# A hybrid decoder layer on one core: one part of the conditioning projection computed at another place, recurrent outputs kept token-major, and the last stage rebuilt

## What is computed

```python
sh1, sc1, g1, sh2, sc2, g2 = split(silu(c) @ w_ada + b_ada)   # six rows of 2048 for each of 9 conditioning vectors
u  = x * (1 + sc1) + sh1
hq, hf, hi, hg, sq, sk, sv = split(u @ w_in)                  # 8 heads of 128 in each group of 1024
o_h, state = hgrn2(silu(hq), f, 1 - f, hi)                    # recurrent heads, 32-token chunks in the kernel
o_h = rms_norm(o_h, hg_norm) * silu(hg)                       # mean square over the 128 values of a head
o_s = rms_norm(stick_breaking(sq, sk, sv, cache), sb_norm)
x1 = LayerNorm(ALPHA * x + g1 * (concat(o_h, o_s) @ w_o))
u2 = x1 * (1 + sc2) + sh2
y  = LayerNorm(ALPHA * x1 + g2 * experts(u2))                 # two of 32 SwiGLU experts for each token
```

## Time and profile before

| | |
|---|---|
| median of 3 runs | 1797.02 us (1795.12 to 1797.27) |
| the profiled execution | 1795.09 us, of which the span from first to last instruction is 1793.3 us |
| TensorE busy (matmuls) | 1591.6 us, 89% of the span |
| VectorE, ScalarE, GpSimd busy | 562.4, 183.6 and 115.3 us |
| moved by DMA | 536.87 MB, mean 299 GB/s |
| granted TensorE clock, mean | 0.951 of full speed |

### The profile page before, as it was taken

One profiled execution on the slowest core, in us unless ns is written; L12 is line 12 of the kernel. 1 busy time (PEld: TensorE's weight loads), 2 busy tenths in 40 slices (PEclk: granted clock), 3 DMA queues, 4 the chain that ended last, 5 costly groups with the idle time before them and its releaser, 6 DMA issues.

```text
span 1793.3 us, 24360 instructions
## 1 busy us (share of the span) xinstructions
PE 1591.6 (89%) x9319; PEld 964.3 (54%) x9319; DVE 562.4 (31%) x988; ACT 183.6 (10%) x298; POOL 115.3 (6%) x154
## 2 busy tenths in 40 slices
PE   3679999999999999999958999999999998999871
PEld 0036666634777775567744646464655454545440
DVE  0010009641221224431466132323232313232328
ACT  0000001300000013321025100000000000000002
POOL 3000000000111100000020000000000000000004
PEclk8789999999998989999988999999999999999995
DMA  9998788875442334465424799999999999999961
GB/s 352 421 381 333 308 333 306 325 283 233 131 142 88 130 120 155 142 250 205 141 94 159 314 420 421 421 421 421 421 421 420 421 421 420 421 421 421 420 263 53
DMA packets 82878, 536.87 MB, mean 299 GB/s; under 512 B 11491, under 2 KB 11667, under 8 KB 24018
## 3 DMA queue, kind: packets, MB, share of 16 engines
q1 hardware_dynamic: 74450, 507.62, 70.8%
q0 software_dynamic: 8048, 26.28, 4.4%
q10 hardware_dynamic: 336, 2.36, 0.4%
HBM read 532.87 MB, written 11.80 MB: 304 GB/s over the span
## 4 chain that ended last, share of the span: by engine, by line
PE 64%; DMA 25%; DVE 6%; issue 3%; ACT 1%; SPq 1%; DVEq 0%; ACTq 0%
DMA ring<-w_up 20%; PE ps L607 18%; PE ps L1071 11%; PE ps L863 7%; PE ps L615 6%; DMA ring<-w_ada 5%; PE ps L1090 5%; PE ps L591 4%; PE ps L1053 2%; PE ps L757 1%; PE ps L719 1%; PE ps L622 1%; DVE arena L1851 1%; SPq L386 1%; PE ps L738 1%
## 5 line engine op out<-in xcount | busy, mean ns | idle before, releaser
L1071 PE MATMUL ps<-ring,arena 128*64 128x256 f32 x3200 | 355.1, 380 | 9.9 <-DMA ring<-w_up 7.7
L607 PE MATMUL ps<-arena,ring 128*128 128x288 f32 x1280 | 325.2, 413 | 0.0
L1071 PEld LDWEIGHTS ps<-ring,arena 128*64 128x64 f32 x3200 | 266.8, 137 | 103.4 <-DMA ring<-w_up 18.4
L607 PEld LDWEIGHTS ps<-arena,ring 128*128 128x128 f32 x1280 | 242.9, 192 | 91.1 <-issue 25.5
L1090 PE MATMUL ps<-arena 128*64 128x512 f32 x800 | 177.2, 594 | 23.5 <-DVE arena L1862 23.5
L591 PE MATMUL ps<-ring,silu_c 128*32 128x512 f32 x768 | 113.2, 698 | 56.3 <-DMA ring<-w_ada 30.7
L1090 PEld LDWEIGHTS ps<-arena 128*64 128x64 f32 x800 | 66.2, 137 | 118.4 <-issue 90.5
L1053 PE MATMUL ps<-arena 64*128 64x512 f32 x400 | 108.1, 636 | 24.1 <-DVE arena L1851 14.9
L863 PE MATMUL ps<-arena,ring 128*128 128x288 f32 x512 | 125.5, 407 | 0.0
L1858 DVE TENSOR_TENSOR arena<-arena,ps 128x256 f32<-128x256 f32 x25 | 10.5, 422 | 342.4 <-PE ps L1071 342.4
L615 PE MATMUL ps<-ring,arena 128*128 128x512 f32 x256 | 114.6, 595 | 1.3 <-DVE arena L1430 1.3
(11 more groups left out here) (400 smaller groups left out, 1220.9 us busy)
## 6 DMA issues: line engine op xcount, KB each, us to landing
ring<-w_gate SPq DMA_DIRECT2D x100, 1024.0 KB, 23.5
ring<-w_up SPq DMA_DIRECT2D x100, 1024.0 KB, 26.4
arena<-w_down SPq DMA_DIRECT2D x100, 1024.0 KB, 20.3
ring<-w_ada SPq DMA_DIRECT2D x96, 1024.0 KB, 8.7
ring<-w_in SPq DMA_DIRECT2D x56, 1024.0 KB, 6.4
ring<-w_o SPq DMA_DIRECT2D x32, 512.0 KB, 6.6
ring<-cache_k SPq DMA_DIRECT2D x16, 512.0 KB, 3.8
ring<-cache_v SPq DMA_DIRECT2D x16, 512.0 KB, 4.0
```

The costliest lines, as they stand in the source:

```text
L607: last = mm(ps[:, bank, 0:T], ring[:, slot, P * t:P * (t + 1)], uT[:, t, :], start=(t == 0), stop=(t == KC - 1))
L1071: last = mm(ps[B * s:B * (s + 1), 2 + c // 4, 0:256], xgT[:, 4 * (c % 4) + t, :], ring[:, c, 512 * t + 256 * s:512 * t + 256 * (s + 1)], s ...
```

## The change

- **g2 moved.** The sixteen chunks of w_ada's sixth part leave the loop of stage 1. SP loads them after w_o's chunks, ahead of expert 0's; TensorE multiplies eight of them after the first LayerNorm's sums, four after the router, four after u2 is turned (`g2_chunks`). The bias rows `bg2` are loaded later. The four pairs of `select_g2` become one run of eight products after the gather lists, with 64 and 32 weight columns instead of 128 and 32.
- **Recurrent outputs token-major.** Queries are now the weights (32 columns in column strip 32*c4), states and values the moving side, into banks 6 and 2. ACT squares with accumulation (`hsum`), DVE scales to `otok`, and TensorE turns the result (`turn_out`): half 0's in the first pass of half 1, half 1's between the key tiles. `heads_out` on DVE applies norm weight and gate. The normalisation leaves the stick-breaking passes.
- **End rebuilt.** The sums start from ALPHA * x1 instead of zero; a block's output is multiplied by g2 when it leaves PSUM (DVE, two products a block; ACT copies both halves unscaled for the sample rows). The last block is taken out of the loop on each engine: its gate and up chunks 0 to 3, then `combine` of the block before, then chunks 4 to 7, down, and a spreading of its own, whose adds also give row sums; ACT gives the sums of squares about a mean guessed before. Sample tokens stay in four quadrants to the end. ln2's rows are loaded by SP behind the last weights, and SP issues the eight stores.

The diff, cut to its core (removed lines mostly left out, since the functions before stand above):

```diff
+        N_MIX, N_SQ, N_SV, N_V = 2 * KC, 2 * KC + 80, 2 * KC + 96, 2 * KC + 112
+        N_G2 = N_V + 24
+        N_END = N_G2 + KC
...
+            for c in range(SLOTS):
+                put(used(N_ROWS + c - SLOTS), c, w_in[3, c])
...
+            for t in range(KC):
+                put(used(N_G2 + t - SLOTS), t % SLOTS, w_ada[5, t])
...
+            sp.wait_ge(u2_stored, 3 * 16)
+            sp.dma_start(ln2b, ln2.partition_broadcast(P)).then_inc(late_loaded, 16)
...
+            pool.wait_ge(hnorm_dve, 6)
+            for j in range(4):
+                pool.dma_start(bg2[32 * j:32 * j + 32, :], b_g2[j].partition_broadcast(32)).then_inc(bg2_loaded, 16)
...
-                for t in (2 * c, 2 * c + 1):
-                    n = N_MIX + 3 * MIX + 3 * c + t % 2
-                    ada_chunk(n % SLOTS, loaded(n), t, 5)
-                n = N_MIX + 3 * MIX + 3 * c + 2
+                n = N_ROWS + c
...
+            def turn_out(half):
+
+                for tt in range(2):
+                    pe.wait_ge(htok_dve, 3 * half + tt + 1)
+                    for h in range(4):
+                        last = nc.tensor.transpose(ps[:, (6, 2)[tt], P * h:P * (h + 1)], otok[tt][:, h, :], ident[:])
+                    last.then_inc(hturn_pe, 1)
+                pe.wait_ge(htok_dve, 3 * half + 3)
+                nc.tensor.transpose(ps[:, 3, P:2 * P], osr, ident[:]).then_inc(hturn_pe, 1)
...
+                        if half == 1:
+                            turn_out(0)
...
+                    if half == 1 and c == 0:
+                        pe.wait_ge(hnorm_dve, 3)
...
+                pe.wait_ge(u_dve, 8 * half + 8)
+                for tt in range(2):
+                    for h in range(4):
+                        k = heads[h]
+                        o = ps[:, (6, 2)[tt], P * h:P * (h + 1)]
+                        for c4 in range(4):
+                            mm(o[CH * c4:CH * (c4 + 1)], abuf[:, tt, k, CH * c4:CH * (c4 + 1)],
+                               tok[:, 3 + tt, P * k:P * (k + 1)], start=True, stop=(4 * tt + c4 == 0),
+                               tile_position=(0, CH * c4))
+                        for c4 in range(4):
+                            c = 4 * tt + c4
+                            if c == 0:
+                                continue
+                            last = mm(o[CH * c4:CH * (c4 + 1)], hq[:, k, CH * c:CH * (c + 1)], shist[:, c - 1, h, :],
+                                      start=False, stop=True, tile_position=(0, CH * c4))
                     last.then_inc(hgo_pe, 1)
...
                 if i == 2:
+                    turn_out(1)
...
+                    pe.wait_ge(hnorm_dve, 6)
                 else:
-                    pe.wait_ge(hrs_act, c)
+                    pe.wait_ge(z_dve, c)
...
-                pe.wait_ge(z_dve, c + 1)
-                pe.wait_ge(hsq_act, c + 1)
-                mm(ps[:, 2, 0:T], ones[:], hsq, start=True, stop=True).then_inc(hrms_pe, 1)
...
+            def g2_chunks(ts):
+
+                for t in ts:
+                    ada_chunk(t % SLOTS, loaded(N_G2 + t), t, 5)
+
+            pe.wait_ge(ss_dve, 5)
+            g2_chunks(range(8))
+
...
+            g2_chunks(range(8, 12))
             for n in range(12):
                 turn_tokens(n, u2T)
+            g2_chunks(range(12, KC))
...
-            for j in range(2, 4):
-                select_g2(j)
-
...
+            pe.wait_ge(tt_act, 24)
+            pe.wait_ge(rows_copied, 6)
+            for j in range(4):
+                r = slice(32 * j, 32 * j + 32)
+                h = j // 2
+                mm(ps[B * h:B * (h + 1), 6 + j % 2, :], rowsel[r, 0:B], ada_rows[r, :], start=True, stop=True,
+                   tile_position=(32 * j, B * h))
+                last = mm(ps[r, 5, :], rowsel[r, P:P + TS], ada_rows[r, :], start=True, stop=True,
+                          tile_position=(32 * j, 32 * j))
+            last.then_inc(g2_pe, 1)
...
-                with pe.If(i < nblocks):
+                with pe.If(i < last_block):
...
+            pe.wait_ge(x_copied, nblocks)
+            for c in range(8):
+                gate_or_up(c, last_block)
+                if c == 3:
+                    combine(last_block)
+            turn_hidden(last_block)
+            for q in range(4):
+                pe.wait_ge(moe_loaded[8 + q], last_block * 16 + 16)
+                for nn in range(2):
+                    last = down(q, nn)
+                    if q == 3:
+                        last.then_inc(last_down, 1)
...
+            def last_tile(i, nn, banks):
+                for r in range(2):
+                    rows = slice(B * r, B * (r + 1))
+                    last = mm(ps[:, banks[r], :], spread[rows, P * i:P * (i + 1)], yout[rows, 512 * nn:512 * (nn + 1)],
+                              start=True, stop=True, tile_position=(B * r, 0))
+                last.then_inc(last_comb, 1)
...
+            pe.wait_ge(last_dve, 1)
+            last_tile(0, 0, (0, 1))
+            last_tile(1, 0, (2, 3))
+            pe.wait_ge(last_act, 2)
...
+            pe.wait_ge(last_dve, 2)
+            last_tile(0, 1, (6, 7))
+            pe.wait_ge(last_sum, 1)
+            last_tile(1, 1, (0, 1))
...
+                act.wait_ge(os_pe, 4 * (half + 1))
+                if half == 1:
+                    act.wait_ge(htok_dve, 3)
+                A(osr, ps[:, 3, 0:P], ACT.Square, accum_out=hsum[:, 2, 0:1])
+                for tt in range(2):
+                    act.wait_ge(hgo_pe, 2 * half + tt + 1)
+                    for h in range(4):
+                        last = A(otok[tt][:, h, :], ps[:, (6, 2)[tt], P * h:P * (h + 1)], ACT.Square,
+                                 accum_out=hsum[:, tt, h:h + 1])
+                    link(last)
+                    n = 4 if tt == 0 else 5
+                    s = hsum[:].rearrange("p a b -> p (a b)")[:, 4 * tt:4 * tt + n]
+                    link(A(s, s, ACT.Ln, bias=epsr[:, 0:1], scale=1.0 / P))
+                    A(s, s, ACT.Exp, scale=-0.5).then_inc(hsum_act, 1)
...
-                act.wait_ge(hrms_pe, c + 1)
-                if c >= 1:
-                    act.wait_ge(hnorm_dve, c)
-                link(A(hrs, ps[:, 2, 0:T], ACT.Ln, bias=epsr[:, 0:1], scale=1.0 / P))
-                A(hrs, hrs, ACT.Exp, scale=-0.5).then_inc(hrs_act, 1)
...
+            act.wait_ge(g2_pe, 1)
+            nc.scalar.copy(g2h, ps[:, 6:8, :].rearrange("p a n -> p (a n)"))
+            nc.scalar.copy(g2q, ps[:, 5, :]).then_inc(g2_act, 1)
...
+            act.wait_ge(tt_act, 24)
+            for q in range(4):
+                ins = nc.scalar.copy(x1q[32 * q:32 * q + 32, :], x1s[:, 512 * q:512 * (q + 1)])
+            ins.then_inc(x1q_act, 1)
...
-                    nc.scalar.copy(yout[:, 0:512], ps[:, 5, :]).then_inc(y_evac, 1)
-
-
+                    nc.scalar.copy(yout_s[:, 0:512], ps[:, 5, :]).then_inc(bank5_act, 1)
+                    act.wait_ge(bank6_dve, i + 1)
+                    nc.scalar.copy(yout_s[:, 512:1024], ps[:, 6, :]).then_inc(y_evac, 1)
...
+            def heads_out(half):
+
+                heads = slice(4 * half, 4 * half + 4)
+                for tt in range(2):
+                    dve.wait_ge(hturn_pe, 3 * half + tt + 1)
+                    v.scalar_tensor_tensor(hout[:, heads, P * tt:P * (tt + 1)],
+                                           ps[:, (6, 2)[tt], :].rearrange("p (h t) -> p h t", h=4), normw[:, 0:1],
+                                           hg[:, heads, P * tt:P * (tt + 1)], ALU.mult, ALU.mult).then_inc(hnorm_dve, 1)
...
+                for tt in range(2):
+                    dve.wait_ge(hsum_act, 2 * half + tt + 1)
+                    v.tensor_tensor(otok[tt], ps[:, (6, 2)[tt], :].rearrange("p (h v) -> p h v", v=P),
+                                    bc(hsum[:, tt, :], 2, P), ALU.mult).then_inc(htok_dve, 1)
+                v.tensor_scalar(osr, ps[:, 3, 0:P], hsum[:, 2, 0:1], None, ALU.mult).then_inc(htok_dve, 1)
...
+                if i == 2:
+                    heads_out(1)
...
-                dve.wait_ge(hrs_act, c + 1)
-                link(v.scalar_tensor_tensor(hout[:, c, :], hout[:, c, :], normw[:, 0:1], hrs, ALU.mult, ALU.mult))
-                v.tensor_tensor(hout[:, c, :], hout[:, c, :], hg[:, c, :], ALU.mult).then_inc(hnorm_dve, 1)
...
+            dve.wait_ge(bg2_loaded, 16 * 4)
+            copy_rows_out(used(N_G2 + KC - 1), 5, bg2[:])
...
-                    v.tensor_copy(yout[:, 512:1024], ps[:, 6, :]).then_inc(y_evac, 1)
-            add_up(nblocks)
...
+                    v.tensor_tensor(yout[:, 512:1024], ps[:, 6, :], g2h[:, 512:1024], ALU.mult).then_inc(bank6_dve, 1)
+                    dve.wait_ge(bank5_act, i + 1)
+                    v.tensor_tensor(yout[:, 0:512], ps[:, 5, :], g2h[:, 0:512], ALU.mult).then_inc(y_evac, 1)
...
+            for i in range(2):
+                last = v.tensor_reduce(guess[:, i:i + 1], moe_out[i], AX, ALU.add)
+            link(last)
...
+            hidden(last_block)
```

(25 more changed lines are left out.)

399 lines of the change are left out of this document (195 added, 204 removed).

## The result

The changed kernel takes 1749.94 us in the median (1747.75 to 1750.18) beside 1796.07 for the kernel before; the ratio is 0.9743 (95% interval 0.9727 to 0.976). Its profiled execution has a span of 1747.8 us beside 1793.3, 45.5 less. The prediction was 1745.5 with a range of 1733 to 1761.

A forecast was written before the change was run, and what follows sets the result against it. TensorE was taken to bound the stages before LayerNorm, DMA the expert blocks, chain length routing and end. Terms sum to -51.5: profiled 1795.09 becomes 1743.6, median 1745.5 us, range 1733 to 1761.

The forecast's parts named there:

- Stage 1: Before the recurrent outputs: removing g2's chunks saves 14.8 us, a longer DVE wait takes 1.7 back; -13.1.
- up to 1.5: Stage 1: the gain would be up to 1.5 us less if the longer gap lowers TensorE's clock.
- Recurrent outputs: Both halves' output products in the new form without ACT's stops: -12.4 and -6.5, together -19 us.
- L910: Recurrent outputs: profile row of the same product shape, 0.059 us each, used to price 60 products at 3.6 us.
- 2.3 put for accumulation and clock: Half 1's recurrent outputs: allowance for squaring with accumulation and the clock after gaps, from nothing to 5.3 us.
- Stick-breaking: Stick-breaking passes: each loses the ones product L833 and a wait on L1209; -8.4 us in all.
- Start of the experts: LayerNorm to first block: eight chunks ahead of ranking and eight serial selecting products, about 15 us, delay the block; +12.6.
- rival of overlapped selection: Start of experts: selecting products overlap or run at 2.4 GHz, about 7.7 us instead of 15; 1738 us, chance 0.18.
- the first block at about 1007: Sign of being right in the changed profile: first expert block starts at 1006.9 instead of 994.28 us.
- Blocks: 24 expert blocks: added DVE product and ACT copy hide under the next block's eight chunks; cost nothing, block still 29.7 us.
- Empty trips and tail: Kernel's end: sixteen empty trips, 9.6 us, neither gained nor lost; tail behind the final combine 24.5 against 47.5, -23.
- rival of a late last block: Last block: combine's adds and guess reductions delay the hidden rows, 7 us with slower small steps; 1752 us, chance 0.10.

The follow-up runs named there:

- sorted sizes: Changed kernel with only the order of its eight selecting products changed, the four of 32x32 weights first, then the four of 32x64; median 1742.79 us.
- three products: Changed kernel with its eight selecting products replaced by three of 128x128 block weights holding the same ones and zeros; median 1739.0 us.
- the cover's run: Changed kernel with one unused DVE reduction, about 8.7 us, added to each looped block's output evacuation between the two g2 products; median 1746.4 us.
- the late combine: Changed kernel with the last block's combine behind chunk 7 instead of chunk 3; first chunk to end 65.9 us instead of 55.5.

## Why the prediction was right, and where its reasons were not

The time fell inside the range and 4.4 us above the point. The profiled execution is 6.1 above its forecast of 1743.6; the difference is luck, since the median stood 0.2 above it and not the 1.9 that were added. The size of nearly every term held, but two held for reasons that the runs took away.

- *Stage 1* (-13.1, measured -10.9). The gap grew to 3.0 as worked out. The term left out of the sum was the clock behind it, put at "up to 1.5": it was 1.7. The runs show that it comes with the longer gap (eight of ten traces, none of four with the short one), but not every time.
- *Recurrent outputs* (-19, measured -20.5). L910 was the right row: 3.6 us. The reason given, that ScalarE's copies made TensorE pause and so lose its clock, is wrong. The old form loses it with no pause at all. The trace of before already said so; TensorE there, ahead of its first wait for a copy at 537.06:

```profile
531.13 0.47 PE L752 MATMUL ps<-arena 128*128 128x128 f32 x2
...
532.34 0.77 PE L752 MATMUL ps<-arena 128*128 128x128 f32 x2
```

  The same products take 0.47 and, 1.2 us on, 0.77: the clock has fallen. In half 1 the chain from the first output product to the cache pages (L814, before L780) took 11.6 us where 12.0 were summed, and of the 2.3 put for accumulation and clock 1.7 came, all of it clock: L814 and the value products behind it run at 1.2 GHz at first.
- *Stick-breaking* (-8.4, measured -8.2): right step by step.
- *Start of the experts* (+12.6, measured +14.5). The 15 us for selection were right, but the reason, that products which share output strips run in a row, is not the cause: alternating tile sizes is. The rival of overlapped selection was dismissed for this kernel rightly and for a wrong reason, and one change of order makes it true. The missing 2 us are L1069 at 1.2 GHz (6.90 instead of 4.36), which the prediction took "as today". Its sign "the first block at about 1007" leaves out the 41.1 us that its own terms gain ahead of it; with them it is 965.8, and 970.2 was measured.
- *Blocks* (0, measured +2.0). About 1 us is the first block's chunks at the lower clock (16.30 instead of 14.04): in the runs with sorted sizes and with three products, where these chunks take 14.0, the 24 blocks take 713.5 and 713.2 instead of 714.3. The other 1 us, against 712.3 before, stays open; the cover's run shows only that the chain of the evacuation is not its cause.
- *Empty trips and tail* (-23.3, measured -23.4). The tail is right. Ahead of it two errors nearly cancel: the sixteen trips took 7.75 and not 9.6, and the four chunks behind them 8.48 and not half of the 14.0 put for eight, since the clock fell. The last block's guess is covered by 0.35 us; the rival of a late last block was closer than its chance of 0.10 says, and the late combine shows its price, 10.4.
- *Not predicted*: +1.3 between the passes and LayerNorm. In sample attention a gap of 1.01 us appears inside a run of 128 products that had none, put down to "issue" (TensorE waited for nothing that the profile shows); it is 0.7 to 2.7 in the eleven other runs with the new form of the outputs, always at the same place, give or take one instruction. In each of the twelve traces the DMA queue for instructions moves one block of 0.02 MB 2.3 to 2.7 us before the gap ends (here at 756.9, and the products go on at 759.34). So TensorE probably waited for its own next instructions, which the prediction has no term for; no run isolates it.

So the gain is the tail's 22 and the outputs' and passes' 29; what the move of g2 gained in stage 1 (10.9) the start of the experts more than gave back (14.5, of which 6.8 by the order of the selection).

## What to carry to other kernels

Small products that use parts of the array ran side by side here only while the tile size stayed the same: sort them by size before thinking about where else to put them. The cheapest edit (an order of eight instructions) gave 6.8 us in its stretch, where moving sixteen megabytes of weights gave 2 to 3. A gap or a stretch of thin products costs its length and often what the clock loses behind it as well, so look at the rows after a gap as well as at the gap. When work is moved into idle time, follow each buffer that it holds: chunks that TensorE uses late free their slots late, and the loads behind them become the next bound.

## What the runs showed of the hardware

Eight products of 32 rows on 512 columns took 14.9 us with alternating 32x32 and 32x64 weights and 3.7 us sorted by size, both at 1.2 GHz.

TensorE's clock fell from 2.4 to 1.2 GHz in windows where the engine was busy 2.00 of 2 us, with 128x128 weights for 32 columns each, and did not fall with 32-column weights for 128 columns. In the changed kernel it stayed at 1.2 GHz through the 14.9 us of selecting products, one at a time, and the 8.7 us of 128x128 products on 128 columns behind them; in the run with three products of 128 rows on 512 columns it was back during the third (1.86, 1.91, 1.18). Behind the same gap of 4.15 us the clock fell in all twelve traces, but not at the same moment: the same eight transposes took 1.97 in some and 1.09 in others. In the two programs whose transposes follow without a gap they took 1.09. This is one source of the 7 us by which programs with the same code there reach LayerNorm apart (up to 2.8 of them between 348 and 438); the gap in sample attention, 0.7 to 2.7, is another, and whether they are all was not isolated.

An empty trip of the block loop took 0.48 us in the changed kernel and 0.60 before, and lay on the path in both.
